# Two out stages of a one-core transformer kernel: the last quarter of the residual rows turned on VectorE instead of TensorE

## The reference

```python
def first_block(x, ...):
    ...
    x = x + jnp.concatenate([ha, hb], axis=-1) @ w_out[i]
    h = rms_norm(x, ffn_norm_g[i])
    u = h @ w_up[i]
    a, g = jnp.split(u, 2, axis=-1)
    a = causal_dwconv(a, conv_w[i], conv_b[i])
    x = x + (jax.nn.gelu(a, approximate=False) * g) @ w_down[i]
    ...

def second_block(x, ...):
    ...
        x = x + merged @ w_out[l]
        x = x + swiglu(rms_norm_2(x, norm_ffn[l]), w_gate_up[l], w_down[l])
    return rms_norm_2(x, norm_final)
```

## Time and profile before

| | |
|---|---|
| median of 3 runs | 2553.18 us |
| lowest and highest run | 2553.04 and 2553.64 us |
| span of the profiled execution | 2551.8 us |
| TensorE busy in it | 2541.6 us |
| VectorE busy in it | 1769.9 us |
| ScalarE busy in it | 1211.5 us |

### The profile page before, as it was taken

One profiled execution on the slowest core, in us unless ns is written; L12 is line 12 of the kernel. 1 busy time (PEld: TensorE's weight loads), 2 busy tenths in 40 slices (PEclk: granted clock), 3 DMA queues, 4 the chain that ended last, 5 costly groups with the idle time before them and its releaser, 6 DMA issues.

```text
span 2551.8 us, 35509 instructions
## 1 busy us (share of the span) xinstructions
PE 2541.6 (100%) x11930; PEld 2135.2 (84%) x11930; DVE 1769.9 (69%) x2642; ACT 1211.5 (47%) x1502; POOL 73.0 (3%) x123
## 2 busy tenths in 40 slices
PE   9999999999999999999999999999999999999998
PEld 7889998888888888888887778888888888888887
DVE  6666668788787875556978866666757676765444
ACT  5545545555555544445544444444544444444443
POOL 2000000000000000001011100000000000000000
PEclk9999999999999999999999999999999999999999
DMA  7666656766666665666666556665666666666664
GB/s 218 192 179 169 163 179 189 204 189 189 192 193 189 190 198 186 199 194 195 198 177 180 169 188 192 195 192 184 197 193 190 196 189 197 189 195 205 199 193 156
DMA packets 359369, 483.79 MB, mean 190 GB/s; under 512 B 22984, under 2 KB 170640, under 8 KB 359024
## 3 DMA queue, kind: packets, MB, share of 16 engines
q1 hardware_dynamic: 352768, 476.13, 62.4%
q0 software_dynamic: 2112, 5.31, 0.9%
q10 hardware_dynamic: 4400, 1.19, 0.2%
HBM read 480.41 MB, written 2.14 MB: 189 GB/s over the span
## 4 chain that ended last, share of the span: by engine, by line
PE 96%; DVE 2%; issue 0%; ACT 0%; POOLq 0%; POOL 0%; DVEq 0%; ACTq 0%
PE acc L1600 27%; PE acc L1602 27%; PE acc L1601 27%; PE acc L1828 3%; PE X L1828 3%; PE X L1835 2%; PE acc L1835 2%; PE acc L1884 1%; PE acc L1883 1%; PE acc L1882 1%; DVE wlo L903 1%; PE X L1971 0%; PE X L1709 0%; PE T L1722 0%; DVE qkt_s L928 0%
## 5 line engine op out<-in xcount | busy, mean ns | idle before, releaser
L903 DVE TENSOR_TENSOR wlo<-raw,whi 128x1024 fp32r<-128x1024 f32 (+1 forms) x916 | 1099.6, 1205 | 675.6 <-ACT whi L512 671.8
L512 ACT ACTIVATE whi<-raw 128x1024 fp32r<-128x1024 f32 (+1 forms) x916 | 947.5, 1043 | 1037.4 <-PE acc L1602 867.4
L1600 PE MATMUL acc<-whi,xt 128*128 128x512 f32 (+1 forms) x1824 | 701.4, 385 | 1.1 <-DVE wlo L903 0.8
L1602 PE MATMUL acc<-whi,xt 128*128 128x512 f32 (+1 forms) x1824 | 696.0, 382 | 0.0
L1601 PE MATMUL acc<-wlo,xt 128*128 128x512 f32 (+1 forms) x1824 | 695.8, 381 | 0.0
L1600 PEld LDWEIGHTS acc<-whi,xt 128*128 128x128 f32 x1824 | 342.5, 188 | 63.7 <-DVE wlo L903 1.7
L1602 PEld LDWEIGHTS acc<-whi,xt 128*128 128x128 f32 x1824 | 342.3, 188 | 61.5
L1601 PEld LDWEIGHTS acc<-wlo,xt 128*128 128x128 f32 x1824 | 342.5, 188 | 60.6
L1600 PE MATMUL acc<-whi,ht_hi 128*128 128x512 f32 x616 | 239.7, 389 | 0.0
L1602 PE MATMUL acc<-whi,ht_lo 128*128 128x512 f32 x616 | 239.7, 389 | 0.0
L1601 PE MATMUL acc<-wlo,ht_hi 128*128 128x512 f32 x616 | 239.6, 389 | 0.0
(11 more groups left out here) (323 smaller groups left out, 2288.1 us busy)
## 6 DMA issues: line engine op xcount, KB each, us to landing
raw<-in_w_up_dram SPq DMA_DIRECT2D x176, 512.0 KB, 3.8
raw<-in_w_down_dram SPq DMA_DIRECT2D x176, 512.0 KB, 4.3
raw<-in_w_gate_up_dram SPq DMA_DIRECT2D x176, 512.0 KB, 4.3
raw<-in_w_in_dram SPq DMA_DIRECT2D x256, 256.0 KB, 3.3
raw<-in_w_out_dram SPq DMA_DIRECT2D x64, 512.0 KB, 3.8
raw<-in_w_in_dram SPq DMA_DIRECT2D x64, 512.0 KB, 3.7
raw<-in_w_in_dram SPq DMA_DIRECT2D x128, 192.0 KB, 3.0
raw<-in_w_ple_gate_dram SPq DMA_DIRECT2D x32, 512.0 KB, 4.8
```

The lines of the kernel that those rows point to most:

```text
L512: act.activation(whi[:, s, :, 0:w.width], raw[:, s, :, 0:w.width], ACT.Copy).then_inc(hi_made, 1)
L903: dve.tensor_tensor(wlo[:, s, :, 0:w.width], raw[:, s, :, 0:w.width], whi[:, s, :, 0:w.width].bitcast(F32), ALU.subtract).then_inc(lo_made, 1)
L1600: pe.matmul(out_, h_, wh_, start=(j == 0 and kk == 0), stop=False)
L1602: done = pe.matmul(out_, l_, wh_, start=False, stop=(j == w.n - 1 and kk == KS - 1))
```

## The change

In both places the last 512 columns take the way of the other three. On VectorE all four parts of the block transposes (16 instructions) stand directly behind `add`, behind stage 3; `split_blocks` and `mean` stand behind stage 6. On ScalarE `split_blocks` stands behind stage 6. TensorE has no `turn` there any more, and before stage 6 it waits for `blocks_lo` and not for the PSUM bank. The rest of the diff is bookkeeping: counts of semaphores, and the functions that are no longer used. Stages "gate" and "mix" keep their turn on TensorE.

```diff
@@ ScalarE, residual @@
                 if n == NB - 1:
-                    after[5] = [lambda: split(phase, dst, gain)]
+                    after[6] = [lambda: split_blocks(phase, n, dst, gain)]
@@ VectorE, residual @@
                 after = {3: [lambda: add(n, w)]}
-                if n < NB - 1:
+                if final:
+                    after[3] += [lambda q=q: turn_part(q, phase, of_x(n), acc_read[w.par], 2 * w.block + 2) for q in range(P // B)]
+                    after[6] = [lambda: split_blocks(phase, n, dst_hi, dst_lo, gain), lambda: mean(phase)]
+                else:
                     after.update(turn_parts(phase, n, of_x(n), acc_read[w.par], 2 * w.block + 2))
...
                     after[2] = [lambda: split_blocks(phase, n - 1, dst_hi, dst_lo, gain)]
-                if final:
-                    after[4] = [lambda: mean(phase)]
-                    after[5] = [lambda: split(phase, dst_hi, dst_lo, gain)]
                 return after
@@ TensorE @@
                 ready = {2 * n: [lambda n=n: pe.wait_ge(blocks_lo, BLOCKS0[phase] + n + 1)] for n in range(NB)}
-                if phase != "down":
+                if phase in RES0:
                     ready[2 * NB - 2] = [lambda: pe.wait_ge(bank_read[T2], USE0[T2][phase] + 1)]
...
-            def residual(phase, w):
-                return {2: [lambda: turn(of_x(NB - 1), phase, acc_read[w.par], 2 * w.block + 2)]}
...
-                ffn(up, 0, splits_ready(before), residual(before, w_last))
+                ffn(up, 0, splits_ready(before), {})
```

More of the change, by code:

```diff
@@ L92, in sandwich_kernel @@
         "fox": (FH // 2, 16, 2, (FH, FH, FH, FH)),
-        "out": (NB // 2, 16, 1, (1, 1, 0, 0)),
+        "out": (NB // 2, 16, 1, (0, 0, 0, 0)),
         "up": (FF // W, 16, 1, (0, 0, FF // W, FF // W)),
@@ L99, in sandwich_kernel @@
         "mix": (2 * NB, 12, 1, (1, 1, 0, 0)),
-        "out2": (NB // 2, 16, 1, (1, 1, 0, 0)),
+        "out2": (NB // 2, 16, 1, (0, 0, 0, 0)),
         "up2": (FF // W, 16, 1, (0, 0, 0, 0)),
@@ L154, in proj_windows @@
         return [Window("proj", 0, n, 1, n % 2, pair=n // 2) for n in range(NB)]
-    RES0 = {"out": NB, "gate": NB + 1, "mix": NB + 2, "out2": NB + 3}
-    BLOCKS0 = {"out": 0, "down": NB - 1, "gate": 2 * NB - 1, "mix": 3 * NB - 2, "out2": 4 * NB - 3}
+    RES0 = {"gate": NB, "mix": NB + 1}
+    BLOCKS0 = {"out": 0, "down": NB, "gate": 2 * NB, "mix": 3 * NB - 1, "out2": 4 * NB - 2}
     B = 32
@@ L1858, in ffn, with hidden_then_down @@
                     multiply(g, xt_hi, xt_lo)
-            def hidden_then_down(up, down, before, w_last, extra={}):
-                ffn(up, 0, splits_ready(before), residual(before, w_last))
+            def hidden_then_down(up, down, before, extra={}):
+                ffn(up, 0, splits_ready(before), {})
                 with pe.Fori(1, FF // W) as i:
@@ L1914, in p_turn @@
                 done.then_inc(p_turned, 1)
-            hidden_then_down("up", "down", "out", ws[-1], {5: [p_turn]})
+            hidden_then_down("up", "down", "out", {5: [p_turn]})
             pe.wait_ge(bank_read[X1], USE0[X1]["down"] + 1)
@@ L2016, in _ @@
                 multiply(ws[n], mt_hi, mt_lo)
-            hidden_then_down("up2", "down2", "out2", ws[-1])
+            hidden_then_down("up2", "down2", "out2")
         @block.gpsimd
```

## The result

| | kernel before | kernel after |
|---|---|---|
| median, device us | 2553.44 (5 runs, 2553.04 to 2554.80) | 2562.71 (5 runs, 2561.75 to 2564.02) |
| profiled execution, its span | 2551.8 | 2561.0 |
| its own time | | 2562.68 |

The ratio is 1.0037, with a 95% interval of 1.0024 to 1.0049: 9.3 us slower, where 5.2 us were forecast, and above the upper end of the range (2561.2).

The account below looks back on a forecast made before the run. TensorE's own work was taken as the bound. Turn removed and stops added gave +2.48 us at A and +2.71 at B, together +5.2 on 2553.18, so 2558.4 us, range 2556.5 to 2561.2.

Parts of the forecast that it names:

- The turn: Removing it from TensorE saves 0.87 us at A (first window of "up") and 0.89 at B (first of "up2").
- The stops: TensorE waits before stage 4 for lo(4), queued behind sixteen transposes on VectorE: 3.35 us at A, 3.60 at B.
- the prediction's last part: Expected signs: 7.2 us of transposes ahead of lo(4) at both places, TensorE waits of about 3.2 and 3.5 us.
- The clock: Rival: TensorE's clock halves behind the stops at A and B; 2564.0 us, or 2561.2 at one place; chance 0.12.
- The prediction's own sign of being wrong: Wrong if TensorE's L903 waits stay below 1 us, clock drops below 1.00, or "up" window two stops over 1 us.
- the case of one fall: The smaller clock case: TensorE's clock falls behind the stop at one place alone, 2561.2 us.
- The row and the loads: Second window of "up": VectorE waits 1.6 us for the row, counted as nothing; late rival 2559.2 to 2560.2, chance 0.22.
- Not slower: Rival: VectorE has lo(4) done in time at A and B, leaving only the turn's saving, 2551.4 us; chance 0.03.

Follow-up runs that it names:

- run with one transpose: Kernel after with one of the sixteen transposes kept at each place, so most of the last 512 turned columns are not computed; 2551.55 us.
- stops filled: Kernel after with 14 extra unused matmuls behind stage 3 of the first window of "up" and 15 in that of "up2"; 2558.91 us.
- three groups and one: Kernel after with the fourth group of four transposes moved from before lo(4) to behind it at both places; 2560.25 us.

## Why the prediction was wrong, and where it was right

**The turn** (-0.87 and -0.89): right. The run with one transpose measures -0.87 and -0.91.

**The stops**: right in size. Sixteen transposes took 7.19 and 7.18 us for 7.17 forecast. With the clock held up, A and B cost 2.58 and 2.80 for 2.48 and 2.71. The waits themselves, 3.19 and 3.46 us, are the 3.2 and 3.5 of the prediction's last part. The first begins at 455.4, where 455.7 was forecast; the second begins at 1839.6 instead of 1838.3, later by what the clock cost at A. Had the clock stayed, the time would have been 2558.9 instead of the 2558.4 forecast.

**The clock**: this is the step that failed. The sum had no term for it; what stood behind each stop was put at full speed, and the runs show 1.5 us at A and 2.8 us at B, 4.3 us together, as much as lies between the forecast and the measured time (2558.4 and 2562.7). As a rival it was there, at 2.8 us for each place (one stage at the lower level): right at B, where the low clock covered more than a stage, and too much at A. Its chance was wrong: 0.12, for something that then happened at both places. The prediction's own sign of being wrong, a granted clock below 1.00 behind a stop, is what the trace shows. The argument against it was that each stop stands alone in hundreds of microseconds of dense work. The trace of after refutes just that: TensorE is 99% busy over the span, and a single stop of 3.2 us was enough at A. The dense work before it did not keep the clock up. I had noted that no row shows the clock in a stop of over 1.2 us, and then still let the rows from short stops speak for long ones, with the range ending at the case of one fall. The rule that the prediction took from the Trainium skill, page "TensorE: Matmul & The Clock Gate", section "Part 1: The HAM clock gate", is that the clock falls to half once the engine has idled for a while and is given back only after sustained work. The trace agrees: the clock is at 0.50 for 3.4 us at A and for 6.8 us at B, and rises while TensorE works.

**The row and the loads**: right for this kernel, and for a reason that was not quite the one given. VectorE waited 1.91 us for the row (1.6 forecast):

```profile
481.43 1.22 DVE L1255 TENSOR_TENSOR a_s<-a_s,rstd_row 128x1024 f32<-128x1024 f32 x1 [1.91 <-DMA rstd_row<-rstd_scratch]
```

No third stop followed. But in the kernel after the clock had held TensorE back 1.5 us more, which widened the cover. With the stops filled and the clock up it was thin and still held: lo(5) was done at 483.49, and TensorE came to it at 483.97. With shorter stops, and with GpSimd held up, it was gone, and the stop was 2.9 us. That GpSimd always stores 2.4 us behind the sum of squares was a step taken from one row; with three groups and one it was 4.7 us. The runs of that kernel spread over 3.5 us.

**Not slower**: out, as forecast; the transposes take 0.45 us each, and 0.25 was the point from which that rival decides.

## What to carry to other kernels

When TensorE is the bound, a stop costs its length and, from some length on, the slow stretch behind it: here nothing at up to 1.6 us, sometimes something at 2.3 to 2.6 us, and 1.5 to 2.8 us more in every profiled stop of 2.9 to 3.5 us. So of a stop of that size the fall of the clock is the main case and not a side case; one long run of moved work should be cut into pieces behind separate products, and where a stop can't be avoided, matmuls into a free bank are cheap (3.8 us gained here with 14 and 15 of them; 4 of them did not suffice at A). And work that an engine off the critical path takes over also delays what stands behind it there, here a small store and the loads behind it: when one stop is removed, ask which transfer was living on its time.

## What the runs showed that was not expected

- A slow stretch does not have a fixed price: 1.5 us of loss behind 3.19 us of standing still, 2.8 us behind 3.46 us, 1.5 us behind 2.89 us, 1.9 us behind 2.30 us. At A the clock was still at 1.00 when TensorE started again and fell about a microsecond later, so that the slow part came into the middle of a stage; at B it was at 0.50 from the restart on.
- Stops of 2.30 us (clock fell) and 2.56 us (clock stayed) in one execution.
- The store of 1 KB took 8.8 to 11.0 us to land in the profiles of all these kernels, and while it is on its way the loads of weights beside it fall from over 300 GB/s to between 23 and 99 GB/s for 6 us and more (61, 42 and 23 GB/s from 460 to 466 in the kernel before). With the store issued at 461.8 and 455.8 a stop of 0.95 and 0.8 us followed, each time of another stage, by a load; with the store at 467.4 it was the row itself that came late, and the stop was 2.9 us. With the store at 456.5, 460.3, 464.6, 464.7, 464.9 or 465.2, in the other kernels, no stop followed.
- GpSimd's first instruction on two numbers per row took 3.36 us instead of 1.09 us when three of VectorE's products ran one behind the other beside it.
